# Values of the recurrence and of the chunk MLP computed with the tokens as standing operand and four weight tiles moving

## The reference, cut to what matters

```
u, v, q, k, vv, r, af, ab, ga, gb = split(h @ w_in)
# two directions of a gated recurrence over chunks, with q, k, vv and gates from af, ab
o = scan_forward(q, k, vv, lf) + flip(scan_backward(flip(q), flip(k), flip(vv), flip(lb)))
b = rmsnorm_heads(o) * silu(r)
# chunk MLP: mixes the 128 tokens of a chunk, per group of 128 channels
a = gelu(u) * (w_spatial @ layernorm(gelu(v)) + b_spatial)
y = (sigmoid(ga) * (a @ w_branch_a) + sigmoid(gb) * (b @ w_branch_b)) @ w_out
```

## Time and profile before

| | |
|---|---|
| three runs | 3276.3, 3277.59, 3278.8 us (median 3277.59) |
| span of the profiled execution, first to last instruction | 3275.0 us |
| busy in the span | PE 98%, weight loads 80%, DVE 58%, ACT 43%, POOL 12% |
| mean granted clock of PE | 0.993 of full speed |
| stage 1 on PE | about 105.2 to 288.1 us |
| stage 2 on PE | from 288.1 us to about 684.8 us |

### The profile page before, as it was taken

One profiled execution on the slowest core, in us unless ns is written; L12 is line 12 of the kernel. 1 busy time (PEld: TensorE's weight loads), 2 busy tenths in 40 slices (PEclk: granted clock), 3 DMA queues, 4 the chain that ended last, 5 costly groups with the idle time before them and its releaser, 6 DMA issues.

```text
span 3275.0 us, 39490 instructions
## 1 busy us (share of the span) xinstructions
PE 3205.4 (98%) x14862; PEld 2614.3 (80%) x14862; DVE 1909.3 (58%) x3085; ACT 1408.1 (43%) x2340; POOL 399.7 (12%) x621
## 2 busy tenths in 40 slices
PE   7999999999999999999999999999899999999998
PEld 4888888888888878888888877877666888888886
DVE  5573434456334387777544546567687687776443
ACT  4782222244333243333233376666576443333221
POOL 1121000012100200000010201111222200001011
PEclk8999999999999999999999999999999999999999
DMA  5465444346543433333854444355976433336662
GB/s 229 164 218 175 129 139 129 111 176 227 185 150 100 137 102 112 120 110 116 257 173 127 145 137 138 129 164 162 175 120 161 148 122 110 105 120 201 214 189 71
DMA packets 226765, 490.99 MB, mean 150 GB/s; under 512 B 21520, under 2 KB 84624, under 8 KB 225040
## 3 DMA queue, kind: packets, MB, share of 16 engines
q1 hardware_dynamic: 145536, 296.01, 29.2%
q0 software_dynamic: 81040, 192.45, 18.6%
HBM read 351.54 MB, written 136.84 MB: 149 GB/s over the span
## 4 chain that ended last, share of the span: by engine, by line
PE 82%; DVE 7%; ACT 4%; DMA 4%; issue 3%; POOL 0%; SPq 0%; DVEq 0%; POOLq 0%; ACTq 0%
PE p L300 12%; PE p L302 12%; PE p L301 12%; PE p L2184 12%; PE p L2186 12%; PE p L2185 12%; DMA s_aw<-i_adaT 1%; PE p L3252 1%; PE p L1201 1%; PE p L1191 1%; PE p L1192 1%; PE p L3238 1%; DMA s_qs<-d_q2l 1%; DMA s_ad<-i_ada 1%; DVE s_pr L3324 1%
## 5 line engine op out<-in xcount | busy, mean ns | idle before, releaser
L300 PE MATMUL p<-s_xh,s_wh 128*128 128x512 f32 x2256 | 900.1, 399 | 9.5 <-DVE s_tmp L420 5.4
L302 PE MATMUL p<-s_xh,s_wl 128*128 128x512 f32 x2256 | 880.6, 390 | 0.0
L301 PE MATMUL p<-s_xl,s_wh 128*128 128x512 f32 x2256 | 879.8, 390 | 0.0
L300 PEld LDWEIGHTS p<-s_xh,s_wh 128*128 128x128 f32 x2256 | 424.4, 188 | 107.4 <-issue 11.1
L302 PEld LDWEIGHTS p<-s_xh,s_wl 128*128 128x128 f32 x2256 | 424.2, 188 | 90.3
L301 PEld LDWEIGHTS p<-s_xl,s_wh 128*128 128x128 f32 x2256 | 424.8, 188 | 86.7 <-issue 1.9
L2184 PE MATMUL p<-s_xh,s_wh 128*128 128x512 f32 x1152 | 449.6, 390 | 1.5 <-DVE s_wl L2433 1.4
L2186 PE MATMUL p<-s_xh,s_wl 128*128 128x512 f32 x1152 | 448.2, 389 | 0.0
L2185 PE MATMUL p<-s_xl,s_wh 128*128 128x512 f32 x1152 | 448.2, 389 | 0.0
L259 DVE TENSOR_TENSOR s_wl<-s_ws,s_wh 128x1024 fp32r<-128x1024 f32 x155 | 190.7, 1241 | 229.7 <-ACT s_wh L251 229.4
L2184 PEld LDWEIGHTS p<-s_xh,s_wh 128*128 128x128 f32 x1152 | 216.2, 188 | 48.4 <-issue 3.6
(11 more groups left out here) (402 smaller groups left out, 5072.5 us busy)
## 6 DMA issues: line engine op xcount, KB each, us to landing
d_h<-s_fhl POOLq DMA_DIRECT2D x80, 512.0 KB, 3.0
s_ws<-i_Wf SPq DMA_DIRECT2D x48, 512.0 KB, 4.3
s_qb<-i_Wf SPq DMA_DIRECT2D x40, 512.0 KB, 4.0
s_qb<-i_Wf SPq DMA_DIRECT2D x80, 256.0 KB, 3.0
s_ws<-i_Wf SPq DMA_DIRECT2D x80, 256.0 KB, 2.7
s_aw<-i_adaT SPq DMA_DIRECT2D x32, 512.0 KB, 3.7
s_xh<-d_h POOLq DMA_DIRECT2D x16, 1024.0 KB, 11.9
s_xl<-d_h POOLq DMA_DIRECT2D x16, 1024.0 KB, 14.9
```

What stands on the lines that cost most here:

```text
L300: pe.matmul(o, wh, H[:, k, c:c + n], start=(k == 0), stop=False)
L301: pe.matmul(o, wh, L[:, k, c:c + n], start=False, stop=False)
L302: last = pe.matmul(o, wl, H[:, k, c:c + n], start=False, stop=(k == 7))
```

## The change

1. `weight_order` puts q before vv.
2. A second set of weight places, XWH and XWL, in the memory of RES. Tiles 5 to 8 (q), 13 to 16 (second half of vv) and 21 to 24 (second half of v) go there; a tile i is in place (i - 1) mod 4.
3. v and vv are made by groups of four tiles and chunks of 128 tokens (`plan_rows`, `rows_pe`). The tokens' block of 128 x 128 is the standing operand, the same block row of four weight tiles is the moving one, 4 x 128 = 512 columns. The output has tokens on the partitions. ACT copies it to TMP, and POOL stores it. VF, the transposes, their bank and the DVE copies are gone from these two stages.
4. Stage 1 has k (3 jobs), q (8), vv (20) and the first group of v (8): 39 fill jobs, in 4 banks. Stage 2 has the second group of v (8), u (16) and r (16): 40 fill jobs, in 3 banks. The times at which weight tiles are made are written out as a list for stage 1 and the start of stage 2.
5. ACT waits for the last rows job before it first writes the scan's output to RES.

```
-    order += [("k", m) for m in range(4)] + [("vv", m) for m in range(8)] + [("q", m) for m in range(4)]
+    order += [("k", m) for m in range(4)] + [("q", m) for m in range(4)] + [("vv", m) for m in range(8)]
...
+    XWH, XWL = placed(([128, NW, 1024], R, "xwh"), ([128, NW, 1024], R, "xwl"))
...
+    def in_second(i):
+        return 5 <= i < 9 or 13 <= i < 17 or 21 <= i < 25
+    def place(i):
+        return (i - 1) % NW
+    def before_in_place(i):
+        if i < NW or 5 <= i < 9:
+            return []
+        return [used[i - 2 * NW if 9 <= i < 29 else i - NW]]
...
+    def plan_rows(jobs, name, group, banks, dst, key, chunks):
+        i = tile_of[(name, 4 * group + 3)]
+        for chunk, half, c, x, ready in chunks:
+            p = Job(i, name, group, c, 512, half, x, ready, banks[len(jobs) % len(banks)])
+            p.bank_free = bank_free[p.bank]
+            p.mm = mm.at(more("mm"))
+            frees(p, "A")
+            p.kind, p.dst, p.group, p.chunk = "rows", dst, group, chunk
+            p.slot, p.slot_free = take_slot()
+            store_planned(p.slot, (key, group))
+            jobs.append(p)
+        for j in range(4):
+            used[i - j] = jobs[-1].mm
+    def rows_pe(p):
+        H, L = p.x
+        WHg, WLg = (XWH, XWL) if in_second(p.i) else (WH, WL)
+        o = B[p.bank][:, :].rearrange("p (a f) -> p a f", a=4)
+        for t in p.bank_free:
+            PEW.wait_ge(*t)
+        PEW.wait_ge(*w_hi.at(p.i + 1))
+        PEW.wait_ge(*w_lo.at(p.i + 1))
+        for k in range(8):
+            for t in p.ready[k]:
+                PEW.wait_ge(*t)
+            xh, xl = H[:, k, p.col:p.col + 128], L[:, k, p.col:p.col + 128]
+            wh, wl = WHg[:, :, k * 128:k * 128 + 128], WLg[:, :, k * 128:k * 128 + 128]
+            pe.matmul(o, xh, wh, start=(k == 0), stop=False)
+            pe.matmul(o, xl, wh, start=False, stop=False)
+            last = pe.matmul(o, xh, wl, start=False, stop=(k == 7))
+        last.then_inc(*mm.up())
...
+        if p.kind == "rows":
+            POW.wait_ge(*p.ev)
+            po.dma_start(p.dst[p.chunk][:, 512 * p.group:512 * p.group + 512], TMP[:, p.slot, :]).then_inc(*stored[p.slot].up())
...
 # stage 1
-        items += [("vv", m, True, "turned", dV, "v", 1.0, 0) for m in range(8)]
         items += [("q", m, False, "plain", dQ, "q", scale_q, TC) for m in range(4)]
-        jobs = plan_fill(items, [0, 1, 2], 3, parts, vf_free)
+        banks = [0, 1, 2, 3]
+        jobs = plan_fill(items, banks, None, parts, [])
+        of_context = [(j, 0, 128 * j, CTX, xt["c"]) for j in range(2)]
+        for group in range(2):
+            plan_rows(jobs, "vv", group, banks, dV, "v", of_context + token_chunks(2, (0, 1)))
+        plan_rows(jobs, "v", 0, banks, dVm, "vm", token_chunks(0, (0, 1)))
+        for p in jobs:
+            p.make = None
+        for j, upto in ((0, 7), (2, 8), (3, 9), (5, 10), (7, 11), (8, 12), (9, 13), (11, 14), (13, 15), (15, 16), (17, 17),
+                        (21, 18), (23, 19), (25, 20), (27, 21), (31, 22), (33, 23), (35, 24), (37, 25)):
+            jobs[j].make = upto
...
 # stage 2
-        items = [("v", m, False, "turned", dVm, "vm", 1.0, TC) for m in range(8)]
-        items += [("u", m, ...) for m in range(8)] + [("r", m, ...) for m in range(8)]
-        jobs = plan_fill(items, [0, 1], TB, parts, [tr.at(planned["tr"])])
+        items = [("u", m, ...) for m in range(8)] + [("r", m, ...) for m in range(8)]
+        banks = [0, 1, 2]
+        jobs = []
+        plan_rows(jobs, "v", 1, banks, dVm, "vm", token_chunks(0, (0, 1)))
+        for j in range(4):
+            jobs[2 * j].make = 26 + j
+        rows_done = jobs[7].mm
+        jobs += plan_fill(items, banks[2:] + banks[:2], None, parts, [])
...
                             ACW.wait_ge(*o_mm[d].at(2 * (s - 2) + hh + 1))
+                            ACW.wait_ge(*rows_done)
                             ac.activation(RES[:, pair_of(d, s) - 2, hh * 512:hh * 512 + 512], B[OB[hh]][:, :], ACT.Copy).then_inc(*o_copy.up())
```

More of the change, by code:

```diff
@@ L72, in __init__ @@
         self.kind, self.dst, self.off, self.scale = "plain", None, 0, 1.0
-        self.starts, self.turned_before, self.split_before = False, None, None
+        self.turned_before, self.split_before = None, None
         self.slot, self.slot_free = 0, []
+        self.make, self.group, self.chunk = None, None, None
         self.vq, self.vq_free, self.tr, self.tc, self.turn_free = 0, [], None, None, []
@@ L234, in ahead, with high_of, low_of @@
         return min(i + group + 2, i + NW, len(order))
+    def in_second(i):
+        return 5 <= i < 9 or 13 <= i < 17 or 21 <= i < 25
+    def place(i):
+        return (i - 1) % NW
+    def high_of(i):
+        return (XWH if in_second(i) else WH)[:, place(i), 0:cols_of[i]]
+    def low_of(i):
+        return (XWL if in_second(i) else WL)[:, place(i), 0:cols_of[i]]
+    def before_in_place(i):
+        if i < NW or 5 <= i < 9:
+            return []
+        return [used[i - 2 * NW if 9 <= i < 29 else i - NW]]
     def raw_weights(i):
@@ L247, in weights_act @@
             ACW.wait_ge(*raw_weights(i)[1])
[L248 to L251, removed]
+            for t in before_in_place(i):
+                ACW.wait_ge(*t)
+            ac.activation(high_of(i), raw_weights(i)[0], ACT.Copy).then_inc(*w_hi.up())
     def weights_dve(upto):
@@ L343, in plan_fill @@
                 p.kind, p.dst, p.key, p.scale, p.off = kind, dst, key, scale, off
-                p.starts = (col == ps[0][0])
+                p.make = ahead(p.i, 1) if col == ps[0][0] else None
                 if before is not None and before.kind == "turned":
@@ L384, in fill_act @@
     def fill_act(p):
-        if p.starts:
-            weights_act(ahead(p.i, 1))
+        if p.make:
+            weights_act(p.make)
         ACW.wait_ge(*p.mm)
@@ L423, in fill_dve @@
     def fill_dve(p, turn_bank):
-        if p.starts:
-            weights_dve(ahead(p.i, 1))
+        if p.make:
+            weights_dve(p.make)
         if p.split_before:
@@ L453, in fill_sp @@
     def fill_sp(p):
-        if p.starts:
-            weights_sp(ahead(p.i, 1) + NS)
+        if p.make:
+            weights_sp(p.make + NS)
     def ended(*outs):
@@ L786, in done, with token_chunks, stage1 @@
                    mcopy, mcopy_d, mturn, mods, shifted, al_hi, al_lo, wal_hi, wal_lo, cb_silu, ctx_out)
-        return parts, (low_rank, done), gone
-    def stage1(parts, low_rank, gone):
-        (al_hi, al_lo, wal_hi, wal_lo, cm_in, cb_silu, vf_free), done = low_rank
+        return parts, xt, (low_rank, done), gone
+    def token_chunks(first, halves):
+        return [(first + 4 * h + j, h, 512 * h + 128 * j, (XH, XL), XT[h]) for h in halves for j in range(4)]
+    def stage1(parts, xt, low_rank, gone):
+        (al_hi, al_lo, wal_hi, wal_lo, cm_in, cb_silu), done = low_rank
         p1 = ExitStack()
@@ L836, in pe_ @@
                 if what == "fill":
-                    fill_pe(jobs[j], 3)
+                    fill_pe(jobs[j], None)
                 elif j < 24:
@@ L900, in dve_ @@
                 if what == "fill":
-                    fill_dve(jobs[j], 3)
+                    fill_dve(jobs[j], None)
                 else:
@@ L969, in stage2 @@
         old_banks = [list(t) for t in bank_free]
-        items = [("v", m, False, "turned", dVm, "vm", 1.0, TC) for m in range(8)]
-        items += [("u", m, False, "plain", dU, "u", 1.0, TC) for m in range(8)] + [("r", m, False, "plain", dR, "r", 1.0, TC) for m in range(8)]
-        jobs = plan_fill(items, [0, 1], TB, parts, [tr.at(planned["tr"])])
+        items = [("u", m, False, "plain", dU, "u", 1.0, TC) for m in range(8)] + [("r", m, False, "plain", dR, "r", 1.0, TC) for m in range(8)]
+        banks = [0, 1, 2]
[5 more added lines that the diff above has]
+        jobs += plan_fill(items, banks[2:] + banks[:2], None, parts, [])
         def direction(d):
@@ L1208, in pe_ @@
                 elif what == "fill":
-                    fill_pe(jobs[w], TB, (4, 8) if w >= len(jobs) - 4 else (0, 8))
+                    fill_pe(jobs[w], None, (4, 8) if w >= len(jobs) - 4 else (0, 8))
                 else:
@@ L1231, in dve_ @@
                 if what == "fill":
-                    fill_dve(jobs[w], TB)
+                    fill_dve(jobs[w], None)
                 elif what == "scan":
@@ L1992, in new_unit @@
             u = Plan()
[L1993 removed]
+            u.i, u.slot, u.src, u.ready, u.kind, u.n = len(units), (2 * place(first_tile) + len(units)) % 8, src, ready, None, None
             u.hi, u.lo = u_hi.at(u.i + 1), u_lo.at(u.i + 1)
@@ L3577, in program @@
     cb = alloc(p1, [128, 1024], F, "cb")
-    parts, low_rank, gone = stage0()
-    gone = stage1(parts, low_rank, gone)
+    parts, xt, low_rank, gone = stage0()
+    gone = stage1(parts, xt, low_rank, gone)
     p1.close()
```

14 lines of the change are left out of this document (8 added, 6 removed).

## The result

The changed kernel takes **3291.11 us** (median of four runs, 3289.25 to 3294.07). The kernel before, run on the same chip, takes 3278.20 (four runs, 3276.30 to 3279.07). The ratio is 1.0040, with a 95% interval of 1.0028 to 1.0052: slower by 12.9 us. The forecast was 3292.

The account below looks back on a forecast made before the run. PE's own work was taken to bound the kernel. Savings of 17.4, new waits of 30.2 and clock 1.4 summed to +14.2; with the profiled 3275.0 and 2.6 to the median, 3292 us, range 3284 to 3298 (53%).

Parts of the forecast that it names:

- Stage 1: Stage 1 about 33 us longer: 43.8 for eight jobs moved in, less 10.4 saved.
- small hold-ups: Stage 1: 3.4 us left over after its listed work; 2.5 of them taken as gained.
- rival 3: Stage 1's side work binds, modulation loads and ACT within 1 us of PE's pace: +5 to +10, 3297 to 3302; 6%.
- The four-run operand: New row jobs' moving operand, four runs of 128 columns from four weight tiles: taken as 0, far end +175 us.
- rival 4: New row jobs: the moving operand in four runs costs time, 10 ns each giving +9 us, 3301; far end +175; 4%.
- Order of weights, places, lookahead: Weight tiles made in time, places reused without waits, stores moving as many bytes: all at 0, far end +3 us.
- The moved cover: Stage 2, scan over 40 jobs: eight waits of 2.6, six of 1.3, one of 1.8 us; 30.2 taken, ends 20 and 40.
- The clock: Stage 2: granted clock falls after one in eight long waits, 1.4 us per fall: 1.4 us, ends 0 and 11.
- rival 2: Stage 2: every long wait trips the clock, 11 to 16 us in place of 1.4: 3301 to 3306; 13%.
- about 21 us shorter: Sign for a right forecast: stage 2 about 21 us shorter and not 51.
- Rival 5: Stage 2: stalls as found but half as long, +15 in place of 30, no clock: about 3275, no change; 11%.
- Rival 1: Stage 2: the scan's chain is still hidden in 40 jobs, so only the 17.4 us saving counts: 3260; 13%.

Follow-up runs that it names:

- 5-3-1: Changed kernel, stage 2's scan steps dealt at 2.5 per fill job, lead 1, so every second gap holds scan steps 5, 3, 1: 3259.50 us, ratio 0.9940.
- 4-2-5: Changed kernel, stage 2's scan steps dealt at 2.5 per fill job, lead 1.5, so every second gap holds scan steps 4, 2, 5: 3263.29 us, ratio 0.9955.
- 2-5-3: Changed kernel, stage 2's scan steps dealt at 2.5 per fill job, lead 0, so every second gap holds scan steps 2, 5, 3: 3276.89 us, ratio 0.9992.
- 1-4-2: Changed kernel, stage 2's scan steps dealt at 2.5 per fill job, lead 0.5, so every second gap holds scan steps 1, 4, 2: 3305.99 us, ratio 1.0083.

## Why the prediction was right, and where it was off

The mechanism held, and the time came within 1 us of the forecast. Part of that agreement is two errors that offset each other.

- **PE is the bound; what is taken from it is gained at its start-to-start time.** Right. vv by rows, alone, gave 11.3 us, with a wait and a fall of the clock of its own in it; the terms for it were 1.1 + 6.8 + 2.5 = 10.4. v by rows gave 7.3 by the medians and 7.1 by the traces; the term was 7.0.
- **Stage 1** grew by 31.4 us where 33.4 was forecast: the saving was 12.4 in place of 10.4. Of the 2.0 us between, 0.9 would be the rest of the 3.4 us of small hold-ups, which no row shows one by one. The other 1.1 is the price of a job: the sum took 5.47 us, from one job at the start of stage 1, and the 36 jobs of 512 columns take 5.44 (36 x 0.03 = 1.1). No wait on a decay bank appeared: rival 3 fell, and so did its +5 to +10.
- **The four-run operand.** The value taken, 0, is right; rival 4 fell with the spacing of 0.22 to 0.23 us.
- **Order of weights, places, lookahead at 0.** Right: no wait of PE in stage 1, and 5-3-1 carries all of it.
- **The moved cover**, 30.2. The waits are where both written-out orders put them, eight and six and one. Priced by the periods they are 8 x 2.6 + 6 x 1.15 + 1.9 = 29.6: the three prices were 2.6, 1.3 and 1.8. That the spreading makes them, and not the row jobs, is shown by the kernel before with the scan over 40 jobs.
- **The clock**, the mis-sized term: 1.4 us, for one fall in eight. In the profiled execution it fell behind three of eight, at 1.6 each: 4.7. What failed is the step "one in eight", which placed 2.37 us between one row at 2.74 and one at 1.91 and leaned to the latter. It did not fall each time either, so rival 2 is out too. Nor does the premise hold that the estimate leaned on, that the clock falls behind the longer idle times and holds behind the shorter ones (last section). The number of falls is that of one execution. The instructions ahead of stage 1 are the same in the orders of the experiments, and over 0 to 102 us the table by stretch has a granted clock of 0.88 in 4-2-5 and 1.00 in 2-5-3, so the clock is not the same in each execution; of the four runs of the changed kernel the profiled one is the longest, by 2.7 to 4.8 us. How many falls the median run had is not shown.
- **The sum.** For both stages: 31.4 - 15.9 = +15.5, forecast +14.2. The difference of 1.3 is 3.3 for the clock, less 2.0 in stage 1, less 0.6 in the waits, with 0.6 us left over. The two profiled spans are 17.8 us apart. What is left of that lies ahead of stage 1 (-0.4) and behind stage 2 (+2.7), where the kernels make the same products, and the medians are 12.9 apart. One number among the signs was worse than the time: stage 2 was to be "about 21 us shorter". The prediction's own terms give 43.8 + 7.0 - 30.2 - 1.4 = 19.2, and it was 15.9.
- **Rival 5, stalls half as long**, fell: the eight waits cost 2.6 us each and the six 1.15.
- **Rival 1, the cover holds**, 3260 us, was wrong for this order, and its arithmetic is right for another: 5-3-1 takes 3259.5 with the same 40 jobs. What it decided on, products done within 0.9 us of the gap's start, was the wrong condition to ask of every order. One in which step 1 ends a gap, with a whole job before step 2, doesn't need it.

## What to carry to other kernels

Where dependent steps are interleaved with fill work, write out by hand which steps share a gap, before and after, and price each pair by when its input is ready: with the same instructions, the orders here span 46 us, and the choice of the lead alone makes a loss of 0.8% (1-4-2) or a gain of 0.6% (5-3-1). Moving fill work out of such a stretch is worth checking for what it was covering, even when the work itself gets cheaper. And if the clock may fall behind idle time of some length, take the number of falls from several places and several executions rather than from one place on either side.

## What the runs showed of the hardware that was not expected

The same idle time of 2.37 us, with PE busy before and behind it, let the granted clock fall in 3 of 8 cases (the changed kernel), 5 of 14 (1-4-2) and 5 of 8 (the kernel before with the scan late). Each fall cost about 1.6 us: jobs' matmuls 0.43 us apart, then back at 0.23. A shorter one of 1.86 us in stage 2 did it once (at 332.53 in 4-2-5), where 1.90 (the changed kernel, at 332.08) and 1.91 did not; and for the 14 waits of about 1 us in 2-5-3 the sum in the table leaves no room for a fall. A later stage has longer ones. In its timeline of PE, 4-2-5, the execution in which 1.86 us was enough, has 2.81 us of idle time and no fall:

```profile
2201.88 0.50 PE L319 MATMUL p<-s_xh,s_wh 128*128 128x512 f32 x1 [2.81 <-DVE s_tmp L476]
2202.21 0.39 PE L320 MATMUL p<-s_xl,s_wh 128*128 128x512 f32 x1
```

And 1-4-2 has one of 1.97 us with a fall, the matmuls behind it 0.43 apart:

```profile
2239.68 0.68 PE L319 MATMUL p<-s_xh,s_wh 128*128 128x512 f32 x1 [1.97 <-DVE s_tmp L476]
2240.16 0.63 PE L320 MATMUL p<-s_xl,s_wh 128*128 128x512 f32 x1
2240.59 0.63 PE L321 MATMUL p<-s_xh,s_wl 128*128 128x512 f32 x1
```

So the length of the idle time alone does not decide it; what does was not settled.
